# Feed-forward stage of a decoder layer: seven block products at one level, or at two levels in interleaved pairs

## The reference

```python
x = x + rms_norm(y, norm_mix_post)
h = rms_norm(x, norm_ffn_pre)
u = jnp.square(jax.nn.relu(h @ w_ff_up))        # 1024 -> 4096
return x + rms_norm(u @ w_ff_down, norm_ffn_post)   # 4096 -> 1024
```

## Time and profile before

| | us |
|---|---|
| median of 3 runs | 1932.86 (1932.54 to 1933.94) |
| span of the profiled execution, first to last instruction | 1930.2 |
| feed-forward stage, from the last write of hT to the end of the chain's matmul piece | 1126.76 to 1904.73 |
| TensorE busy in the span | 1834.9 |
| VectorE, ScalarE, GpSimd busy | 728.9, 544.3, 493.8 |

### The profile page before, as it was taken

One profiled execution on the slowest core, in us unless ns is written; L12 is line 12 of the kernel. 1 busy time (PEld: TensorE's weight loads), 2 busy tenths in 40 slices (PEclk: granted clock), 3 DMA queues, 4 the chain that ended last, 5 costly groups with the idle time before them and its releaser, 6 DMA issues.

```text
span 1930.2 us, 25764 instructions
## 1 busy us (share of the span) xinstructions
PE 1834.9 (95%) x10406; PEld 1490.1 (77%) x10406; DVE 728.9 (38%) x1631; ACT 544.3 (28%) x1230; POOL 493.8 (26%) x435
## 2 busy tenths in 40 slices
PE   7999999978999799999889999999999999999997
PEld 6888887845555477777668888888888888888886
DVE  5232211556766565655420353202322232123324
ACT  3311211368877645444410420000000000000002
POOL 3222222324544421221112332222222222222222
PEclk9999999979999899999979999999999999999999
DMA  4011222050000486766531101111111111111112
GB/s 140 22 44 50 75 63 66 7 196 10 7 7 9 171 324 206 272 234 210 188 123 44 45 22 44 44 43 40 45 41 36 40 44 42 44 44 44 44 56 88
DMA packets 120382, 158.10 MB, mean 82 GB/s; under 512 B 21936, under 2 KB 104536, under 8 KB 112008
## 3 DMA queue, kind: packets, MB, share of 16 engines
q1 hardware_dynamic: 111048, 89.34, 15.2%
q0 software_dynamic: 9216, 67.11, 9.6%
HBM read 144.16 MB, written 16.47 MB: 83 GB/s over the span
## 4 chain that ended last, share of the span: by engine, by line
PE 70%; DVE 4%; ACT 2%; issue 2%; POOL 1%; DMA 1%; DVEq 0%; ACTq 0%
PE PS L290 45%; PE PS L1970 8%; PE PS L1774 4%; PE PS L1759 4%; PE PS L1787 3%; PE PS L1980 1%; PE PS L2103 1%; PE PS L1988 1%; PE PS L457 1%; POOL Z L1618 1%; PE PS L2140 1%; DVE Z L389 1%; ACT Z L371 0%; PE PS L2035 0%; PE PS L364 0%
## 5 line engine op out<-in xcount | busy, mean ns | idle before, releaser
L290 PE MATMUL PS<-Z,ring 128*128 128x258 f32 x1152 | 258.2, 380 | 0.0
L290 PEld LDWEIGHTS PS<-Z,ring 128*128 128x128 f32 x1152 | 218.0, 189 | 32.8
L2612 ACT ACTIVATE Z<-PS 128x516 f32<-128x516 f32 x80 | 48.0, 600 | 640.8 <-PE PS L290 640.8
L290 PE MATMUL PS<-hT,ring 128*128 128x258 f32 x960 | 215.4, 381 | 1.3 <-DVE hT L532 1.3
L290 PEld LDWEIGHTS PS<-hT,ring 128*128 128x128 f32 x960 | 181.3, 189 | 29.2 <-DVE hT L532 1.5
L248 POOL TENSOR_TENSOR Z<-ring 128x512 f32<-128x512 f32 x36 | 46.5, 1291 | 609.1 <-PE PS L290 597.2
L290 PE MATMUL PS<-Z 128*128 128x258 f32 x832 | 188.8, 383 | 5.6 <-issue 5.6
L2637 DVE TENSOR_TENSOR Z<-PS,Z 128x516 f32<-128x516 f32 x96 | 66.8, 696 | 312.0 <-PE PS L290 312.0
L290 PEld LDWEIGHTS PS<-Z 128*128 128x128 f32 x832 | 158.7, 191 | 30.6 <-issue 6.3
L290 PE MATMUL PS<-hT,Z 128*128 128x258 f32 x640 | 145.9, 380 | 0.0
L290 PEld LDWEIGHTS PS<-hT,Z 128*128 128x128 f32 x640 | 121.1, 189 | 18.4
(11 more groups left out here) (399 smaller groups left out, 2930.0 us busy)
## 6 DMA issues: line engine op xcount, KB each, us to landing
ring<-in_w_ff_up SPq DMA_DIRECT2D x32, 512.0 KB, 5.0
ring<-in_w_ff_down SPq DMA_DIRECT2D x32, 512.0 KB, 4.1
ring<-in_w_in SPq DMA_DIRECT2D x9, 1024.0 KB, 5.2
X<-in_x_prompt SPq DMA_DIRECT2D x8, 1024.0 KB, 8.6
out_y_prompt<-X SPq DMA_DIRECT2D x8, 512.0 KB
out_win_sample<-in_state_nsa_win SPq DMA_DIRECT2D x1, 4088.0 KB
out_kv_prompt<-Z SPq DMA_DIRECT2D x8, 256.0 KB, 2.0
ring<-in_w_in SPq DMA_DIRECT2D x8, 256.0 KB, 4.3
```

The costliest lines, as they stand in the source:

```text
L290: last = nc.tensor.matmul(M.PS[:, bank_of(M, n, e) + c, 0:CW], a[:, k, :], b[:, k, c * CW:(c + 1) * CW], start=e in (M1, M2, M5) and k == ...
L2612: nc.scalar.activation(halves(place(*tiles(n), e)), bank_view(M, n, e), ACT.Relu if e == M4 and kinds[n] == "up" else ACT.Copy).then_inc(s ...
```

## The change

The stage is rewritten as the class `Nested`: Winograd's seven products at an outer level, on halves of 1024 x 1024 weights and halves of the tokens, and for each of the outer products a chain of seven inner products on quarters. A round g (four, as before) has 14 chains: 7 for the up projection and 7 for the down projection, run as seven stages A to G of two chains P and Q, whose products alternate (M1 of P, M1 of Q, M2 of P, ...; the inner order is M1, M2, M6, M5, M7, M3, M4). An inner product has 4 matmul instructions of 258 columns (2 contraction tiles, 2 column blocks). There are 4 x 14 x 7 x 4 = 1568 matmul instructions in place of 32 x 7 x 8 = 1792. The two chains use different banks, and a bank's next user comes three products later.

What each engine does in a round:

- GpSimd: 8 adds of 512 columns that prepare the inner halves of the weight blocks (IT), 42 that make three inner weight sums for each chain (s2, s3, s4), 8 whole adds of 2048 columns for the outer weight sums (S1 to S4, DS1 to DS4), and 6 of 2064 columns that add the outer temporaries of the down projection into the output sums y (A1X1, A1X4, A5X4, A5X3, A7X4, A7X2). Inner weight sums lie in eight places, so those of a chain wait for products of the chains two and three before it.
- VectorE: 42 adds of 516 columns for the inner data sums (t2, t3, t4), 4 that prepare inner halves of u, 10 of 2064 columns for outer data sums and sums of u (T2H, T3H, T4H, U11, U12, U22, T1U to T4U), and 74 moves out of PSUM with an add (70 in the first round).
- ScalarE: moves M1, M6, M5, M4 of the chains whose place is new (24 a round, 28 in the first), and relu and square of u as two whole passes over each of four quarters.
- SyncE: 8 loads of 1 MB a round into seven places, three of them in X.

Around the stage: x is stored to y_prompt and y_sample in the norm before (nine DMAs) and read back at the end, since X holds weights and sums in between; three fills of y come ahead of the stage on GpSimd; the closing norm turns two tiles instead of three before the last M4 and uses banks 0, 2 and 4; 17 semaphores of the gated-attention stage are cleared and freed before the attention stage starts.

```diff
@@ phase_norms, use 1, SyncE @@
             for s in range(2):
                 dense.wait_product(sp, KD // 2 - 2 + s, M4)
-                for f in range(2):
-                    ...
-            norm.wait_added(sp, norm.order.index(QT))
-            sp.dma_start(O["y_sample"].rearrange("b s d -> (b s) d"), M.Xs).then_inc(stored, 16)
-            sp.wait_ge(stored, 16)
+                nest.load(sp, A, 0, (A11, A12)[s])
+            nest.load(sp, A, 0, A21)
+            nest.load(sp, A, 0, A22)
+            for i in range(NT):
+                norm.wait_added(sp, i)
+                t = norm.order[i]
+                dst = out[t] if t < QT else O["y_sample"].rearrange("b s d -> (b s) d")
+                sp.dma_start(dst, x_tile(M, t)).then_inc(M.sem("x_kept"), 16)
@@ class Nested @@
+    def slot(n, e):
+        return 14 * (n // 2) + 2 * e + n % 2
+    def fresh(n):
+        g, j = divmod(n, RNG)
+        return j in (0, 1, 2, 7, 8, 11) or (j == 9 and g == 0)
+    def by_act(self, n, e):
+        return self.fresh(n) and e in (M1, M6, M5, M4)
+    def bank(self, n, e):
+        turn = 4 * (n // 2 % 2)
+        return (turn if e in (M1, M6, M7, M4) else 4 - turn) + 2 * (n % 2)
@@ phase_ffn, GpSimd @@
+        def sums(g, q):
+            for i in range(3):
+                for f, n in enumerate(chains(g, q)):
+                    x, at = N_.weights(n), 3 * n + i
+                    if at >= 8:
+                        N_.wait_product(pool, (at - 8) // 3, (M6, M7, M3)[(at - 8) % 3])
+                    ...
+                    step(g, f"{letters[q]} s{i + 2}{'PQ'[f]}", pool.tensor_tensor(N_.s(n, i), a, b, ALU.subtract))
+        pool.wait_ge(M.sem("x_kept"), 16 * (QT + 1))
+        pool.wait_ge(hwr, 2 * (QT + 1))
+        for m, t in ((0, 0), (1, 1), (1, 0)):
+            pool.memset(N_.y(m, t), 0.0).then_inc(N_.zero, 1)
+        pool.wait_ge(N_.zero, 3)
+        for g in range(ROUNDS):
+            transform(g, "IT A11", 0)
+            transform(g, "IT A12", 1)
+            sums(g, PA)
+            transform(g, "IT A21", 2)
+            transform(g, "IT A22", 3)
+            whole(g, "S1", 2, 2, 3, ALU.add)
+            if g >= 1:
+                N_.wait_chain(pool, RNG * g - 2)
+            whole(g, "S2", 4, 2, 0, ALU.subtract)
+            sums(g, PB)
+            N_.wait_chain(pool, RNG * g)
+            whole(g, "S3", 0, 3, 4, ALU.subtract)
+            N_.wait_chain(pool, RNG * g + 1)
+            whole(g, "S4", 1, 1, 4, ALU.subtract)
+            sums(g, PC)
+            transform(g, "IT D11", 5)
+            sums(g, PD)
+            transform(g, "IT D21", 2, True)
+            transform(g, "IT D22", 6)
+            whole(g, "DS1", 2, 2, 6, ALU.add)
+            transform(g, "IT D12", 4)
+            N_.wait_chain(pool, RNG * g + 4)
+            whole(g, "DS2", 0, 2, 5, ALU.subtract)
+            N_.wait_chain(pool, RNG * g + 5)
+            whole(g, "DS4", 1, 4, 0, ALU.subtract)
+            sums(g, PE_)
+            N_.wait_out(pool, RNG * g + 7)
+            into(g, "A1X1", N_.y(0, 0), N_.bb(g), ALU.add)
+            into(g, "A1X4", N_.y(1, 1), N_.bb(g), ALU.add)
+            N_.wait_chain(pool, RNG * g + 7)
+            whole(g, "DS3", 5, 6, 0, ALU.subtract)
+            sums(g, PF)
+            N_.wait_out(pool, RNG * g + 8)
+            into(g, "A5X4", N_.y(1, 1), N_.ba(g), ALU.add)
+            into(g, "A5X3", N_.y(1, 0), N_.ba(g), ALU.subtract)
+            sums(g, PG)
+            N_.wait_out(pool, RNG * g + 10)
+            N_.wait_out(pool, RNG * g + 11)
+            into(g, "A7X4", N_.y(1, 1), N_.u(1, 1), ALU.add)
+            into(g, "A7X2", N_.y(0, 1), N_.u(1, 1), ALU.subtract)
@@ phase_ffn, TensorE @@
+        def product(n, e):
+            ...
+            for k in range(2):
+                for c in range(2):
+                    last = nc.tensor.matmul(M.PS[:, N_.bank(n, e) + c, 0:HB], x[:, k, c * P:(c + 1) * P], y[:, k, :],
+                                            start=e in (M1, M2, M5) and k == 0, stop=k == 1, skip_group_check=True)
+            last.then_inc(N_.prod, 1)
+        for g in range(ROUNDS):
+            for q in range(7):
+                for e in range(7):
+                    for f, n in enumerate(chains(g, q)):
+                        if g == ROUNDS - 1 and q == PG and e == M4:
+                            norm.turn(pe, f)
+                        product(n, e)
@@ phase_ffn, VectorE: the place of each long add in its stage (at = 2e + f) @@
+            if q == PA and at == 2:
+                add(a, h(1, 1), h(0, 1), ALU.subtract)
+            if q == PA and at == 6:
+                add(b, a, h(0, 0), ALU.subtract)
+            if q == PB and at == 0:
+                add(u(0, 0), u(0, 0), u(1, 0))
+            if q == PC and at == 0:
+                add(u(0, 1), u(1, 0), u(1, 1))
+            if q == PC and at == 6:
+                add(a, h(1, 0), a, ALU.subtract)
+            if q == PD and at == 0:
+                add(u(1, 1), u(1, 0), u(1, 1))
+            if q == PD and at == 10:
+                add(u(0, 1), u(0, 1), u(0, 0), ALU.subtract)
+            if q == PE_ and at == 6:
+                N_.wait_w(dve, g, "A1X4")
+                add(b, u(1, 1), u(0, 1), ALU.subtract)
+            if q == PE_ and at == 10:
+                add(u(0, 0), b, u(0, 0), ALU.subtract)
+            if q == PF and at == 6:
+                N_.wait_w(dve, g, "A5X3")
+                add(a, u(1, 0), b, ALU.subtract)
+            if q == PG and at == 1 and g + 1 == ROUNDS:
+                N_.wait_w(dve, g, "A7X4")
+                nc.vector.tensor_tensor(y(1, 0), y(1, 0), y(1, 1), ALU.add).then_inc(N_.last, 1)
+            if q == PG and at == 6 and g + 1 == ROUNDS:
+                nc.vector.tensor_tensor(y(0, 1), y(0, 1), y(1, 1), ALU.add).then_inc(N_.last, 1)
```

More of the change, by code:

```diff
@@ L350, in turn @@
         nc, M, n, t = self.nc, self.M, self.toks(i), self.order[i]
[L351 to L359, removed]
+        if self.use == 2:
+            M.nested.wait_last(pe, i)
+        else:
+            last = len(M.dense.kinds) - 1
+            if i == 0:
+                for e in (M3, M7):
+                    M.dense.wait_moved(pe, last, e)
+            if t == (4 if self.early else 0):
+                for e in (M2, M4):
+                    M.dense.wait_moved(pe, last, e)
         if i >= len(self.banks):
@@ L506, in _ @@
                 norm.wait_read(pool, i)
[L507 to L510, removed]
+                wait_x(pool, M, t, 1 + use)
                 pool.tensor_tensor(x_tile(M, t), x_tile(M, t), norm.tmp_of(i), ALU.add).then_inc(norm.added, 1)
@@ L2583, in _, with step, transform, whole @@
     @block_.gpsimd
     def _(pool):
-        for n in range(NP):
-            st.wait_loaded(pool, n)
-            weight_sums(nc, pool, st, pair_slot(M, n), n)
+        def step(g, what, ins):
+            ins.then_inc(N_.w, 1)
+        def transform(g, what, p, second=False):
+            x = N_.place[p]
+            N_.wait_loaded(pool, g, p, second)
+            step(g, what, pool.tensor_tensor(N_.winner(x, 0, 1), N_.winner(x, 0, 1), N_.winner(x, 1, 1), ALU.add))
+        def whole(g, what, out, a, b, op):
+            step(g, what, pool.tensor_tensor(N_.flat[out], N_.flat[a], N_.flat[b], op))
@@ L2589, in _ @@
     @block_.tensor
     def _(pe):
[L2591 to L2595, removed]
[L2596 to L2605 removed]
+        READY_W = ("IT A11", "IT A12", "S1", "S2", "S3", "S4", "IT A22", "IT D11", "DS1", "DS4", "DS2", "DS3", "IT D12", "IT D22")
@@ new lines, in move @@
+        def move(n, e):
+            g, j = divmod(n, RNG)
+            if e == M1:
+                if j in (3, 4, 5, 6):
+                    N_.wait_d(dve, g, {3: "U11", 4: "U12", 5: "U12", 6: "U22"}[j])
+                if j == 9:
+                    N_.wait_w(dve, g - 1, "A7X2")
+                if j == 10:
+                    N_.wait_w(dve, g, "A5X4")
+                if j == 12:
+                    N_.wait_w(dve, g, "A1X1")
+                if j == 13 and g + 1 < ROUNDS:
+                    N_.wait_w(dve, g, "A5X3")
+                if j == 13 and g + 1 == ROUNDS:
+                    dve.wait_ge(N_.last, 1)
+            if e in (M2, M7, M3):
+                N_.wait_read(dve, n, {M2: M1, M7: M5, M3: M6}[e])
+            N_.wait_product(dve, n, e)
+            x = N_.inner_out(n, e)
+            nc.vector.tensor_tensor(x, N_.view(n, e), x, ALU.add).then_inc(N_.dve, 1)
```

457 lines of the change are left out of this document (357 added, 100 removed), and 13 rows, old and new, of tables (DVE_STEPS, POOL_STEPS).

## The result

The changed kernel takes 1945.31 us (median of 4 runs, 1941.77 to 1948.22) against 1933.4 of the kernel before beside it: a ratio of 1.0056, 95% interval 1.0041 to 1.007. It is slower by 0.56%; the forecast was 1928.0. The profiled execution has a time of 1944.09 and a span of 1942.4, against 1930.2.

A forecast was written before the change was run, and what follows sets the result against it. It took TensorE's matmul count in the feed-forward stage as the bound. Terms: -97.7 matmuls, +79 stalls, +6.9 start, +4.7 last G, +1.2 end, +1.0 semaphores = -4.9 us, forecast 1928.0 us; 8 in 10: 1875 to 1970.

The forecast's parts named there:

- What bounds the kernel: Feed-forward stage: only TensorE's number of matmuls counts over 777.93 us; the other engines have 570 to 730 us of slack.
- the matmuls that go: Feed-forward stage: 3584 matmul records become 3136, 97.7 us less; a round without stalls takes 170.9 us.
- the busy times: Per round: VectorE 111 us, GpSimd 125 to 127, ScalarE 30, all below TensorE's 171, so TensorE stays the bound.
- rival 1: Feed-forward stage: the shared port hardly matters and the stalls vanish, giving 1844 us; chance 8%, half the stalls another 12%.
- GpSimd's long add: GpSimd adds of 2048 or 2064 columns: no row showed one; put at 4.53 us, possibly 4 to 9.2.
- The port: VectorE two-SBUF-operand adds and GpSimd adds shut each other out for whole instructions; holds take 165 of 171 us a round.
- The stalls: TensorE waits in stages A to G, walked through in code order: 19.5 us a round, 79 us in all.
- The edges: Both ends of the feed-forward stage: start +6.9 us, last G +4.7, end +1.2; clearing semaphores +1.0.
- clearing the semaphores: Clearing 17 semaphores at the boundary near 398 us: between 0 and 3 us, taken as 1.0.
- The clock: TensorE's granted clock in the stage: no term in the sum, only a rival, in which gaps lose the 2.4 GHz level.
- rival 3: Feed-forward stage: gaps of 2 to 6 us lower TensorE's clock to a mean 0.97, +21 us, 1949 us; chance 10%.
- Rival 2: Feed-forward stage: GpSimd becomes the bound, its work and VectorE's port holds 174 us a round; mean 1955 us, chance 28%.

The follow-up runs named there:

- portfree: Changed kernel with VectorE's two-SBUF-operand adds made one-operand reductions, the second operand left out (result not valid): 1851.6 us, one execution.
- fill: Changed kernel with do-nothing matmuls put into TensorE's gaps in A and B of rounds 2 to 4 and every E: 1933.0 us.
- gaps: portfree with TensorE made to wait twice a round, in C and G, for chains of 2 to 10 small ScalarE copies: 1879.1 us, one execution.
- split4: Changed kernel with each long GpSimd add issued as four pieces of 512 or 516 columns: 1901.7 us, 0.9838 of the kernel before.
- split2: Changed kernel with each long GpSimd add issued as two pieces of 1024 or 1032 columns: 1901.4 us, 0.983 of the kernel before.
- split2late: split2 with T2U and T3U of stage E moved behind the moves of products 11 and 12: 1907.7 us, 0.9853 of the kernel before.
- split2mid: split2 with the order of edges at both ends, and T2U at place 8, T3U at 12 in E: 1894.5 us, 0.9786 of the kernel before.
- edges: Changed kernel with first transforms and block sums ahead of GpSimd's fills, and LX3 behind ten moves of the last G: 1933.1 us.

## Why the prediction was wrong

The direction was wrong. The range held the time, in part by luck: a term left out (some 30 us) and terms put too high (15 us) go against each other. Step by step:

- **What bounds the kernel, the matmuls that go, the busy times.** Right. Products stand 1.741 us apart, forecast 1.744, so a round without stalls is some 170.6, forecast 170.9; portfree, with the port out of play, came to 1851.6 where rival 1's sum gave 1844.
- **GpSimd's long add, which no row showed.** 4.53 us for 2048 columns by the line through 512 and 1024, and 4.57 for 2064 by the same line; portfree, with the port out of play, has 4.55 and 4.57.
- **The port.** Right in mechanism. S1 above keeps two short adds to 5.89 us, and T2H ends 2.2 us behind S2: whole instructions of 2048 columns shut VectorE out. The Trainium skill's rule (SBUF — State Buffer, sections "SBUF: two separate sides" and "Who interferes with whom"), that the port pair is an exclusive lock kept for the whole instruction, agrees with this. So does its other half, that a VectorE instruction with at most one SBUF input, outside the 2-port perf modes, does not contend: 680 ns in portfree, 688 for the moves.
- **The stalls.** The walk found the places; idle time in a steady round against the forecast:

| stage | forecast | measured |
|---|---|---|
| A | 3.4 | 3.3 |
| B | 4.0 | 3.4 |
| C | 0 | 0 |
| D | 6.0 | 5.4 |
| E | 4.5 | 2.4 |
| F | 1.6 | 2.3 |
| G | 0 | 0 |

  79 us with restarts and the last G's 4.7 are 83.7; 67.5 (4.6 of it the last G's) and 3.5 of restarts are 71.0: 12.7 us less. By this term alone the kernel would have been faster than forecast.
- **The edges.** Start 6.9, measured 7.4 over the kernel before; the last G 4.7, measured 4.6; the end 1.2, measured -0.5 (0.8 less for transposes ahead of the last M4, 0.3 more behind it); clearing the semaphores 1.0, but everything ahead of the stage moved by 0.1 alone.
- **The clock: the step that failed.** The sum has no term for it. It stood only as rival 3, at 10%, as if it were another world beside the stalls; but the forecast's own stalls of 3.4 and 4.0 us are what lowers the clock. Measured: some 27 us in the changed kernel, more than rival 3's 21, and 4 to 5 more in what a gap costs beside its idle time and the 0.1. The sum's -4.9, with 12.7 less for the stalls, 2.6 less for the end and the semaphores, 0.5 more for the start and 31.8 for this rest, gives +12.1; the span grew by 12.1. Without the slow clock, by this sum, the span would have shrunk by 15 us: this term alone turned the sign. That rival 3's 1949 lies near the 1945 is luck in part, since its stalls were 12.7 too long. fill shows that the loss goes when the gap is filled, gaps that a gap alone brings it, in two stages and with the port out of play.
- **Rival 2, GpSimd as the bound,** at 28% the heaviest, was not it: a GpSimd add released TensorE once, at the start, and GpSimd was busy for 146 of a steady round's 196 us, the time that VectorE's turns added to its records included, where the rival had 174. Its lateness shows only when its adds are cut: in E and F of split4, in E of split2, in F of split2late and split2mid.

What stays open: why the same gap of 3.3 us costs 0.1, 1.8 or 2.9 at different times. Gaps were made one of each length, in one run, and the cost of the gap in A changed from round to round within one kernel. The D gap in fill says that what went before a gap counts beside its length; what of it was not tried. split4, with as much idle time as split2, loses 9 us more by its clock. Its idle time stands in eight gaps of 3.1 to 6.1 us, all of them with slow products behind (16 us together), where split2 has four of 3.7, one of them with none (7 us together).

## What to carry to other kernels

Price each stall twice: with its own length, and with what the clock loses behind it once it is long. In all the kernels here together, 71 of 81 gaps of 2.4 us and more had 1.4 to 3.3 us of slow clock behind them, 11 of 38 between 1.7 and 2.3 had 1.5 to 1.7, and none of 196 shorter ones had any, so one stall of 3.3 us mostly cost as much as three of 1.7. Where GpSimd shares its port with VectorE, cut its long instructions to the length that the waiting engine's slack can take (two pieces of 1024 columns gave 2.2%), and look next at what now waits for the GpSimd results themselves. Moving VectorE's long steps back did not help here, because the next stage's first move waited for a late GpSimd add; the timeline of the engine that releases TensorE tells which of the two it is.

## What the runs showed of the hardware

- What a gap costs behind itself does not grow in step with its length: in gaps 2.74 us cost 1.7, 4.53 us cost 1.5, and 2.29 cost nothing; the 6.1 us of split4 cost 2.0 to 2.7. In the changed kernel, 11 of 12 gaps of 2.4 us and more cost 1.7 to 2.8 (the one of 2.62 us in the first B nothing), and 2 of 11 between 1.88 and 2.27 us cost 1.6 and 1.7, the others nothing. Longer gaps can be free too: one of 3.72 in split2, one of 3.61 in edges.
- VectorE and GpSimd in turns stretch each other unequally: under the changed kernel the 184 short VectorE adds went from 680 to a mean of 1844 ns (2884 in the worst group), while GpSimd's 2064-column adds went from 4571 to 4789 and its 2048-column ones from 4552 to 5253 (6501 in the worst group).
- A move out of PSUM with one operand in SBUF never noticed any of this: 688, 694 and 686 ns in the changed kernel, portfree and split2.
